# One transformer block pair on one core: the MLP's down projections as pairs of 64-row products on the halves of the TensorE array

## The reference

```python
def _sq_relu_mlp(h, w_up, w_down):
    a = jax.nn.relu(h @ w_up)
    return (a * a) @ w_down
...
        h = h + _sq_relu_mlp(_rmsnorm(h, mlp_norm[i]), mlp_w_up[i], mlp_w_down[i])
```

## Time and profile before

| | |
|---|---|
| median of 3 runs | 2479.44 us (2479.44 to 2479.73) |
| profiled execution | 2480.34 us, of it a span of 2478.4 us from the first to the last instruction |
| TensorE | busy 2465.8 us, 99% of the span |
| VectorE | busy 1585.9 us, 64% |
| ScalarE | busy 1586.3 us, 64% |

### The profile page before, as it was taken

One profiled execution on the slowest core, in us unless ns is written; L12 is line 12 of the kernel. 1 busy time (PEld: TensorE's weight loads), 2 busy tenths in 40 slices (PEclk: granted clock), 3 DMA queues, 4 the chain that ended last, 5 costly groups with the idle time before them and its releaser, 6 DMA issues.

```text
span 2478.4 us, 29766 instructions
## 1 busy us (share of the span) xinstructions
PE 2465.8 (99%) x12403; PEld 2037.2 (82%) x12403; DVE 1585.9 (64%) x1314; ACT 1586.3 (64%) x2107; POOL 33.4 (1%) x41
## 2 busy tenths in 40 slices
PE   9999999999999999999999999999999999999998
PEld 7887788888888888888888888888888888888887
DVE  5865658757647548577765685545666677646675
ACT  6545778836737548776465684535587788638873
POOL 0000000000000000000000000000000000000000
PEclk9999999999999999999999999999999999999999
DMA  8554456455464565545443455555754555555554
GB/s 288 187 189 168 176 189 235 162 201 215 170 231 166 198 222 186 195 178 187 153 155 139 153 187 187 191 199 187 265 192 173 188 200 188 194 196 188 199 190 153
DMA packets 69366, 472.37 MB, mean 191 GB/s; under 512 B 7912, under 2 KB 8352, under 8 KB 13424
## 3 DMA queue, kind: packets, MB, share of 16 engines
q1 hardware_dynamic: 67040, 460.62, 51.5%
q0 software_dynamic: 1312, 7.73, 0.8%
q10 hardware_dynamic: 880, 2.11, 0.2%
HBM read 468.33 MB, written 2.11 MB: 190 GB/s over the span
## 4 chain that ended last, share of the span: by engine, by line
PE 96%; DVE 1%; ACT 1%; DMA 1%; issue 1%; SPq 0%; POOLq 0%; POOL 0%; DVEq 0%; ACTq 0%
PE acc L585 30%; PE acc L586 30%; PE acc L587 30%; DMA w_raw<-in_stream 1%; PE tp L728 1%; PE tp L727 1%; PE tp L729 1%; PE tp L918 1%; PE acc L727 0%; PE acc L728 0%; PE acc L729 0%; PE tp L851 0%; DVE w_lo L1810 0%; PE tp L605 0%; ACT w_hi L1137 0%
## 5 line engine op out<-in xcount | busy, mean ns | idle before, releaser
L1810 DVE TENSOR_TENSOR w_lo<-w_raw,w_hi 128x2048 fp32r<-128x2048 f32 x422 | 965.0, 2288 | 670.7 <-ACT w_hi L1137 668.0
L1137 ACT ACTIVATE w_hi<-w_raw 128x2048 fp32r<-128x2048 f32 x422 | 807.4, 1915 | 453.3 <-DMA w_raw<-in_stream 444.2
L585 PE MATMUL acc<-w_hi,x_hi 128*128 128x512 f32 (+1 forms) x2112 | 825.1, 391 | 2.5 <-DVE w_lo L1817 1.7
L586 PE MATMUL acc<-w_lo,x_hi 128*128 128x512 f32 (+1 forms) x2112 | 818.6, 388 | 0.0
L587 PE MATMUL acc<-w_hi,x_lo 128*128 128x512 f32 (+1 forms) x2112 | 818.6, 388 | 0.0
L585 PEld LDWEIGHTS acc<-w_hi,x_hi 128*128 128x128 f32 x2112 | 396.6, 188 | 87.9 <-DVE w_lo L1817 2.6
L587 PEld LDWEIGHTS acc<-w_hi,x_lo 128*128 128x128 f32 x2112 | 396.5, 188 | 81.5
L586 PEld LDWEIGHTS acc<-w_lo,x_hi 128*128 128x128 f32 x2112 | 396.7, 188 | 80.2 <-issue 1.0
L585 PE MATMUL acc<-w_hi,a_hi 128*128 128x512 f32 x1120 | 436.4, 390 | 0.1
L587 PE MATMUL acc<-w_hi,a_lo 128*128 128x512 f32 x1120 | 435.8, 389 | 0.0
L586 PE MATMUL acc<-w_lo,a_hi 128*128 128x512 f32 x1120 | 435.7, 389 | 0.0
(11 more groups left out here) (436 smaller groups left out, 1677.4 us busy)
## 6 DMA issues: line engine op xcount, KB each, us to landing
w_raw<-in_stream SPq DMA_DIRECT2D x422, 1024.0 KB, 4.8
w_raw<-in_stream SPq DMA_DIRECT2D x16, 256.0 KB, 7.8
raw_T<-in_stream SPq DMA_DIRECT2D x4, 1024.0 KB, 6.9
raw_b<-in_stream SPq DMA_DIRECT2D x4, 1024.0 KB, 8.9
h<-in_x SPq DMA_DIRECT2D x4, 512.0 KB, 14.1
frow<-in_rows POOLq DMA_DIRECT2D x2, 1024.0 KB, 6.1
m_raw<-in_mem_turned POOLq DMA_DIRECT2D x1, 2048.0 KB, 9.7
memt<-in_mem POOLq DMA_DIRECT2D x1, 2048.0 KB, 11.2
```

The source lines that it names most:

```text
L585: pe.matmul(dst, xh, wh[:, k], start=first and k == 0, stop=False)
L586: pe.matmul(dst, xh, wl[:, k], start=False, stop=False)
L1137: act.activation(w_hi[:, c % SLOTS], raw(c), ACT.Copy).then_inc(hi_ready, 1)
L1810: dve.tensor_tensor(low_part(c), raw(c), w_hi[:, c % SLOTS].bitcast(F32), ALU.subtract).then_inc(lo_ready, 1)
```

## The change

Each of the down phases' matmuls over 128 rows becomes two over 64 rows, partitions 0 to 63 and 64 to 127 of both operands. The first half sums up in `acc` as before, the second in a pair of banks of `tp`. VectorE adds both pairs to h, one after the other, and the bank pair is released with the second addition. Before tp is used again in the second block, TensorE waits for the last two of these additions.

```diff
+            def half_rows(blk, half, m):
+
+                return tpf(blk + 1)[:, m * N:(m + 1) * N] if half else acc[:, blk % 2, m]
+
+            def chunk_by_half_rows(c, lhs, k0, blk, first, last):
+
+                pe.wait_ge(lo_ready, ready(c))
+                if first:
+                    accs.wait(pe, blk - 2)
+                wh = w_hi[:, c % SLOTS].rearrange("p (k n) -> p k n", n=N)
+                wl = low_part(c).rearrange("p (k n) -> p k n", n=N)
+                for k in range(4):
+                    for m in range(M):
+                        xh = lhs[0][:, k0 + k, m * P:(m + 1) * P]
+                        xl = lhs[1][:, k0 + k, m * P:(m + 1) * P]
+                        for half in range(2):
+                            own = slice(64 * half, 64 * half + 64)
+                            pe.matmul(half_rows(blk, half, m), xh[own], wh[own, k], start=first and k == 0, stop=False)
+                        for half in range(2):
+                            own = slice(64 * half, 64 * half + 64)
+                            pe.matmul(half_rows(blk, half, m), xh[own], wl[own, k], start=False, stop=False)
+                        for half in range(2):
+                            own = slice(64 * half, 64 * half + 64)
+                            mm = pe.matmul(half_rows(blk, half, m), xl[own], wh[own, k], start=False, stop=last and k == 3)
+                mm.then_inc(used, 1)
...
-                    chunk(C_MLP + GROUP * g + 19 + c, A, 4 * q, accs.name["down", g, b], q == 0, q == 3)
+                    chunk_by_half_rows(C_MLP + GROUP * g + 19 + c, A, 4 * q, accs.name["down", g, b], q == 0, q == 3)
...
             def dn_side(c):
                 if c == 3:
                     pe.wait_ge(wg_l, 2)
+                    accs.wait(pe, accs.name["down", 3, 2])
+                    accs.wait(pe, accs.name["down", 3, 3])
...
-                        add_to_h(("down", part, n), n, C_MLP + GROUP * part + c)
+                        blk = accs.name["down", part, n]
+                        hn = h[:, :, n * N:(n + 1) * N]
+                        dve.wait_ge(used, C_MLP + GROUP * part + c + 1)
+                        link(dve.tensor_tensor(hn, acc[:, blk % 2], hn, ALU.add))
+                        dve.tensor_tensor(hn, tpf(blk + 1).rearrange("p (m n) -> p m n", m=M), hn, ALU.add).then_inc(accs.sem(blk), 1)
```

## The result

The changed kernel takes 2484.64 us (median of 16 runs, 2483.92 to 2485.18), the kernel before 2479.61 on the same chips (16 runs): +5.03 us, a ratio of 1.0020 with a 95% interval of 1.0013 to 1.0028. It is slower, clear of the noise but by 0.2% only. The forecast was 2486.2 with a span of 2482 to 2491; of the +6.7 in its sum 5.0 came.

The account below looks back on a forecast made before the run. TensorE, busy 2465.8 of 2478.4 us, was taken as the bound. Pairs +1.5, switches +1.6 and VectorE's second addition +3.6 sum to +6.7 us, forecasting 2486.2 us, range 2482 to 2491.

Parts of the forecast that it names:

- Pairs: Down phases' 1536 pairs of 64-row products: halves overlap at 227.7 ns a pair, 1 ns more than now, +1.5 us.
- the 87.4 to 87.8 that were to show it: Predicted sign: a window over the first down phase should be 87.4 to 87.8 us for 384 pairs.
- The worry about twice the results per us: Argument for the no-overlap rival (6%, 2833 us): fp32r halves deliver twice as many results to PSUM as any row shown.
- Switches: Going in and out of halves, two switches a phase, eight in all: about 0.2 us each, +1.6 us.
- The second addition: VectorE's extra add per down block: hidden in the first three phases, stalls TensorE +3.6 us through the fourth's chain.
- the 3 to 4 that were to show it: Predicted sign: TensorE idle 3 to 4 us for line 1838's low parts, only around 1050 to 1085.
- The second finds VectorE 0.76 idle and makes that 1.75: Fourth phase: the first added addition delays ScalarE by 1.25 us, the second makes it 1.75, third 3.0, fourth 4.25.
- the slack of 0.65: Slack before TensorE needs the low part for the next phase's chunk 2, subtracted from the 4.25 us delay.
- my 1.1: Blocks 0 and 1 of the fourth phase: by the prediction's working, their doubled additions delay by 1.75, costing +1.1 us.
- The bounds of the pair: Limits for a pair of half-row products: 216 ns if the fixed part shrinks, 453 ns with no overlap.

Follow-up runs that it names:

- the same-rows run: Changed kernel with both products of a pair on rows 0 to 63, still into two pairs of banks: 2829.95 us, +350 over the kernel before.
- The kernel with blocks 0 and 1 alone: Kernel before, with VectorE's addition doubled only for blocks 0 and 1 of the fourth down phase: 2480.33 us, +0.65, ratio 1.0003.
- three and three: Changed kernel with a tile's three products of rows 0 to 63 written first, then the three of rows 64 to 127: 2484.77 us.
- with six: Changed kernel with six products of rows 0 to 63 written in a row, then six of rows 64 to 127: 2490.44 us, ratio 1.0045.
- twelve in a row: Changed kernel with twelve products of rows 0 to 63 written in a row, then twelve of rows 64 to 127: 2637.14 us, ratio 1.0637.

## Why the prediction was right, by its steps

**Pairs** (+1.5 in the sum): right in mechanism, 1.5 too high. A chunk of 24 pairs takes the 5.44 us of before; the run without the second addition leaves +0.49 per phase and all of it at the edges. A pair costs 226.7 ns, 0.0 more; the 1 ns of the forecast was read from no row. So the first phase takes 87.29, just below the 87.4 to 87.8 that were to show it. fp32r at its full pace overlaps on halves as fp32 did; the same-rows run shows +350 where it doesn't. The worry about twice the results per us "as anything shown" was larger than the rows allow: the quads of the earlier trace rows give 4 x 256 columns in 215 ns, 4.8 a ns, and a pair here 2 x 512 in 226.7, 4.5. The Trainium skill's page "TensorE: Matmul & The Clock Gate" (Packing small matmuls, The mechanism) has about 4 ns for each further tile; the trace agrees for the distance of the two starts (3 to 4 ns), but it is not added to the interval.

**Switches** (+1.6): 8 x 0.247 = 2.0. The 0.09 ahead and the 0.11 behind were right, and so was charging both at every switch, though the rows showed the one on the way in and the other on the way back. What was missing are the 0.05 spread over the intervals after that. The 0.11 was read with some luck, at a place where the type of the operands changes too. And it is no price of the rows alone: 0.34 in place of 0.23 also stands behind a stop of TensorE for a low part, with 64 rows before and after it (1058.49 to 1058.83, below).

**The second addition** (+3.6, and 0 in the first three phases): 3.1 in the changed kernel (its window is 106.95, less 103.36 and 0.49), 3.3 alone. The place, the chain and the two chunks are as forecast: TensorE idles 1.5 us ahead of line 609 and 1.0 ahead of line 585 between 1040 and 1090, both for VectorE's w_lo, in the grouped lines of the changed kernel:

```profile
L609 PE MATMUL acc<-w_hi,a_hi 64*128 64x512 f32 x41 | 16.0, 389 | 1.5 <-DVE w_lo L1838 1.5
...
L585 PE MATMUL acc<-w_hi,x_hi 128*128 128x512 f32 x28 | 11.1, 397 | 1.0 <-DVE w_lo L1838 1.0
```

These 2.5 us, less than the 3 to 4 that were to show it, count from a product's recorded end, 0.39 behind its start, and leave out the longer intervals after a stop. From start to start the two stops are 1.7 and 1.1 us over the usual 0.23, with 0.15 and 0.12 behind them, 3.1 in all. The first:

```profile
1056.58 0.39 PE L615 MATMUL tp<-w_hi,a_lo 64*128 64x512 f32 x1
1058.49 0.49 PE L609 MATMUL acc<-w_hi,a_hi 64*128 64x512 f32 x1 [1.53 <-DVE w_lo L1838]
...
1058.83 0.39 PE L612 MATMUL acc<-w_lo,a_hi 64*128 64x512 f32 x1
```

The term that was mis-sized is that of the first two additions: "The second finds VectorE 0.76 idle and makes that 1.75". This is the timeline of ScalarE in the changed kernel. The phase starts 0.82 later there and its products another 0.25 (the switch), so 1.07 of each difference from the earlier trace rows is no delay of ScalarE:

```profile
1022.79 3.40 ACT L1204 ACTIVATE sq<-turned 32x256 f32<-32x256 f32 x8 [2.60 <-DVE turned L1881]
...
1028.15 3.40 ACT L1204 ACTIVATE sq<-turned 32x256 f32<-32x256 f32 x8
...
1054.80 3.40 ACT L1204 ACTIVATE sq<-turned 32x256 f32<-32x256 f32 x8 [2.95 <-DVE turned L1881]
```

and of VectorE:

```profile
1024.79 1.22 DVE L2115 TENSOR_TENSOR h<-acc,h 128x1024 f32<-128x1024 f32 x1
1026.04 1.23 DVE L2116 TENSOR_TENSOR h<-tp,h 128x1024 f32<-128x1024 f32 x1
1027.30 1.25 DVE L1881 STREAM_TRANSPOSE turned<-h 128x1024 f32<-128x1024 f32 x1
```

The move at 1028.15 starts before the second block's transpose ends (1028.55): it is the second half of the first block's, and ScalarE turns to the second block only at 1035.00. So the first two additions together delay ScalarE by 1.25, not 1.75; with the third that is 2.5 (1054.80 against 1051.19, less 1.07), and with the fourth 3.75, less the slack of 0.65 is 3.1. The kernel with blocks 0 and 1 alone shows the 1.27 directly. Its +0.82 in the window lies between 0.6 (1.25 - 0.65) and my 1.1 and would not decide it by itself; with the 0.1 to 0.15 behind a stop, 0.7 to 0.8 fits it and 1.2 does not.

**The rest.** Measured terms: 0.0 + 2.0 + 3.1 = 5.1, of 5.03. The forecast's errors (+1.5, -0.4, +0.5) cancelled in part. The bounds of the pair (216 and 453) were both real questions: the upper one is what the same-rows run takes. Why an fp32r product has 13.4 ns beside its columns, halved or not, no run says. No version beats the kernel before: halves leave a pair's price alone, so all that they bring are switches and additions.

## What to carry to other kernels

Cutting a full contraction into halves of the array was free in TensorE's intervals (226.7 ns a pair) and brought nothing there, so its price is what surrounds it: here about 0.25 us for each change between 128 and 64 rows, and the work of summing the halves. On an engine with a third of its time idle that extra work still costs time where its result starts a chain that other queues stand behind; sum the delays along that chain and subtract the slack once. And look at what the waiting instruction in fact reads before adding a delay to it.

## What the runs showed of the hardware

Products on different halves of the rows ran as two streams. With three and three in the written order the time was that of strict alternation (2484.77 against 2484.64), with six it was 5.8 us longer, and only from twelve in a row on were halves left alone (2637), which fits a reach of three products. Two products on the same 64 rows never overlapped, neither into different banks nor in a row into the same ones (226.7 ns each), and a product over half of the rows was no cheaper than over all of them. A change of the rows in use cost 0.25 us, 0.09 of it ahead of the first product and the rest in the intervals behind it, in both directions; similar longer intervals (0.34 and then 0.24, in place of 0.23) stood behind a stop without any change of rows.
